# Startup and stage hand-over of a hybrid attention and SSD layer: x loaded whole, two sets of temporaries, one product order and one load order changed

## The reference, cut to what matters

```
h = rms_norm(x, norm_gain)                       # x: 1024 rows x 1024
proj = h @ w_in                                  # -> q, k, v, z, xBC, dt, gates
o_a = window_attention(q, k, v, ...)             # 16 heads, window of 128
y_s = ssd_mixer(conv(xBC), dt, ...)              # chunks of 64; B and C are part of xBC
branch_a = (o_a * silu(z_a)) @ w_attn_proj
branch_b = rms_norm(y_s * silu(z_s)) @ w_ssd_proj
out = x + (sigmoid(g_a) * branch_a + sigmoid(g_b) * branch_b) @ w_out
```

## Time and profile before

| what | value |
|---|---|
| time, median of 3 runs | 1417.9 us (1417.76 to 1418.82) |
| the profiled execution's own time | 1417.91 us |
| its span in the profile | 1416.1 us |
| PE busy, share of the span | 96% |
| DVE, ACT, POOL busy | 55%, 43%, 41% |
| mean granted clock of PE | 0.986 |

### The profile page before, as it was taken

One profiled execution on the slowest core, in us unless ns is written; L12 is line 12 of the kernel. 1 busy time (PEld: TensorE's weight loads), 2 busy tenths in 40 slices (PEclk: granted clock), 3 DMA queues, 4 the chain that ended last, 5 costly groups with the idle time before them and its releaser, 6 DMA issues.

```text
span 1416.1 us, 20612 instructions
## 1 busy us (share of the span) xinstructions
PE 1358.4 (96%) x7108; PEld 1088.0 (77%) x7108; DVE 782.6 (55%) x955; ACT 612.1 (43%) x1148; POOL 585.1 (41%) x344
## 2 busy tenths in 40 slices
PE   5698999999999979999999999999999999998999
PEld 4686777888888857888787878888768888776787
DVE  4775777676666455536554555555365554555311
ACT  5545444545444343435252535344356533323110
POOL 3443564445544423333333233333336666443321
PEclk9899999999999989999999999999999999999999
DMA  5331644422323276778666785869586265334431
GB/s 201 144 90 66 191 138 134 178 103 99 110 104 119 103 183 157 189 199 157 202 154 203 164 210 151 238 150 202 129 296 235 104 218 196 136 139 158 146 106 59
DMA packets 166500, 221.59 MB, mean 156 GB/s; under 512 B 7760, under 2 KB 127824, under 8 KB 166208
## 3 DMA queue, kind: packets, MB, share of 16 engines
q1 hardware_dynamic: 130640, 172.64, 43.0%
q10 hardware_dynamic: 35728, 48.37, 9.4%
q0 software_dynamic: 96, 0.13, 0.0%
HBM read 152.57 MB, written 63.31 MB: 152 GB/s over the span
## 4 chain that ended last, share of the span: by engine, by line
PE 84%; issue 5%; POOL 3%; DVE 3%; DMA 2%; ACT 2%; SPq 0%; ACTq 0%; POOLq 0%; DVEq 0%
PE F L180 37%; PE F L930 28%; PE F L1772 3%; PE M L1772 3%; PE M L1093 2%; PE M L1136 2%; DMA sb_early<-x_d 2%; POOL sb_res L1596 1%; PE F L1130 1%; PE F L1123 1%; PE F L1107 1%; PE M L1130 1%; PE M L1123 1%; PE F L1725 1%; PE F L899 1%
## 5 line engine op out<-in xcount | busy, mean ns | idle before, releaser
L180 PE MATMUL F<-sb_xb,sb_whl 128*128 128x512 f32 x1536 | 376.3, 402 | 0.0
L180 PEld LDWEIGHTS F<-sb_xb,sb_whl 128*128 128x128 f32 x1536 | 286.9, 188 | 75.2 <-issue 9.2
L192 POOL TENSOR_TENSOR sb_whl<-sb_wst,sb_whl 128x1024 fp32r<-128x1024 f32 x64 | 159.3, 2490 | 405.6 <-ACT sb_whl L189 405.3
L180 PE MATMUL F<-sb_X,sb_whl 128*128 128x512 f32 x1104 | 259.7, 396 | 5.9 <-issue 3.0
L180 PEld LDWEIGHTS F<-sb_X,sb_whl 128*128 128x128 f32 x1104 | 206.5, 187 | 58.5 <-issue 8.2
L930 PE MATMUL F<-sb_tv,sb_whl 128*128 128x512 f32 x1008 | 242.4, 396 | 2.3 <-DVE sb_acc L734 2.3
L930 PEld LDWEIGHTS F<-sb_tv,sb_whl 128*128 128x128 f32 x1008 | 189.2, 188 | 49.3 <-issue 3.1
L414 POOL TENSOR_TENSOR sb_whl<-sb_acc,sb_whl 128x512 fp32r<-128x512 f32 x103 | 145.7, 1421 | 135.8 <-ACT sb_whl L461 135.8
L930 PE MATMUL F<-sb_xb,sb_whl 128*128 128x512 f32 x756 | 187.6, 401 | 7.5 <-POOL sb_whl L414 5.7
L930 PEld LDWEIGHTS F<-sb_xb,sb_whl 128*128 128x128 f32 x756 | 142.7, 190 | 46.3 <-POOL sb_whl L414 7.6
L189 ACT ACTIVATE sb_whl<-sb_wst 128x1024 fp32r<-128x1024 f32 x64 | 67.6, 1058 | 198.4 <-DMA sb_wst<-w_units 97.1
(11 more groups left out here) (216 smaller groups left out, 1776.5 us busy)
## 6 DMA issues: line engine op xcount, KB each, us to landing
sb_wst<-w_units SPq DMA_DIRECT2D x64, 512.0 KB, 5.8
sb_acc<-cs_d SPq DMA_DIRECT2D x8, 2048.0 KB, 20.6
sb_wst<-w_units SPq DMA_DIRECT2D x12, 1024.0 KB, 4.9
x_d<-sb_res ACTq DMA_DIRECT2D x24, 512.0 KB, 2.7
sb_acc<-w_units SPq DMA_DIRECT2D x10, 1024.0 KB, 4.9
sb_acc<-x SPq DMA_DIRECT2D x16, 512.0 KB, 5.1
sb_early<-x_d SPq DMA_DIRECT2D x8, 1024.0 KB, 8.1
sb_acc<-ecs_d SPq DMA_DIRECT2D x16, 512.0 KB, 23.6
```

The lines of the kernel that those rows point to most:

```text
L180: last = nc.tensor.matmul(bank, weight(slot, wp, k), act(ap, k, half), start=(k == 0 and wp == 0 and ap == 0), stop=(k == NK - 1 and wp == 1))
L192: return nc.gpsimd.tensor_tensor(weights(slot, 1), raw_unit(slot), weights(slot, 0).bitcast(f32), ALU.subtract)
```

## The change

1. All eight tiles of x are loaded at once, into the part of `TV` that is written last. A row then lies in pieces of 128 numbers (512 bytes) with a stride, where it was one piece of 4 KB before. The order of the first loads changes too: tile 0, the v weights, dt, then tile 1.
2. `ttmp` becomes two sets, so `b12_copy(q)` waits for `t_lo` of q - 2.
3. Lists of the startup: PE starts the projections one tile later; ACT makes the v weights' high part of unit 0 ahead of the squares of tile 1; the low part of dt moves from POOL to DVE; POOL makes the first product's low part ahead of the last `t_lo`; `combine_x(3)` goes ahead of a `take_dt`, `v_copy(6)` ahead of a `split`.
4. In the last pair only, products 4 and 5 change places. PE's loop is one pair shorter and the last pair is written out.
5. SP's first tile of stage 2 is written out, and `bc` is loaded in it right behind `xb`, ahead of the weight unit and of `csb`. The other tiles keep their order.
6. `state` is cleared by POOL, behind its low parts of the weights, and PE waits for that only ahead of `off(0)`. PE's entry to stage 2 waits for `u2_done` in place of `c12_done`.

```diff
-        xrow, w = carve(acc_all, 2 * NK * VD, 3, DM)
+        ttmp2, w = carve(acc_all, 2 * NK * VD, 4, 4, P)
+        sums, w = carve(acc_all, w, 2, HALF)
...
-        ttmp, _ = carve(part_all, 0, 4, 4, P)
+        ttmp1, _ = carve(part_all, 0, 4, 4, P)
+        ttmp = (ttmp1, ttmp2)
...
+        def order(n):
+            return (0, 1, 2, 3, 5, 4, 6) if n == NPAIR - 1 else range(7)
...
+        def xrow(n):
+            rows = early.rearrange("p a (s k t) -> p (a s) k t", s=2, k=NK)
+            return rows[:, n % 4, :, (2 + n // 4) * P:(3 + n // 4) * P]
...
             load_x(0)
-            load_x(1)
             sp.dma_start(wst[:]..., a["w_units"][V0:V0 + 2]...).then_inc(v_in1, 16)
             sp.dma_start(dtraw[:], ...).then_inc(v_in1, 16)
-            load_x(2)
-            for n in range(3, NT):
-                sp.wait_ge(xt_done, n - 2)
+            load_x(1)
+            for n in range(2, NT):
                 load_x(n)
-                if n == 4:
-                    sp.wait_ge(v_lo, 3)
-                    load_raw(0)
+            sp.wait_ge(v_lo, 2)
+            load_raw(0)
...
             def b12_copy(q):
-                if q:
-                    act.wait_ge(t_lo, q)
+                if q >= 2:
+                    act.wait_ge(t_lo, q - 1)
...
             for q in range(4):
+                if q == 3:
+                    product_low(0, 0)
                 pool.wait_ge(t_hi, q + 1)
...
+                if n == 2:
+                    dve.wait_ge(v_hi, 3)
+                    nc.vector.tensor_tensor(vw[:, 1, :, 2 * P:VD], dtraw[:], vw[:, 0, :, 2 * P:VD].bitcast(f32),
+                                            ALU.subtract).then_inc(dt_lo, 1)
...
             for n in range(NT):
                 transpose_x(n)
-                if n == 1:
-                    pe.wait_ge(v_lo, 3)
-                if n >= 1:
-                    project_vdt(n - 1)
+                if n == 2:
+                    pe.wait_ge(v_lo, 2)
+                    pe.wait_ge(dt_lo, 1)
+                if n >= 2:
+                    project_vdt(n - 2)
+            project_vdt(NT - 2)
             project_vdt(NT - 1)
...
-            with nc.tensor.Fori(0, NPAIR - 8) as i:
+            with nc.tensor.Fori(0, NPAIR - 9) as i:
                 for idx in range(7):
                     product(idx, i, 1, 8)
+            for idx in range(7):
+                product(idx, 0, 0, NPAIR - 1)
...
                 sp.dma_start(xb[:], x_d[0:16, ...]...).then_inc(x2_in, 16)
+                if first:
+                    sp.wait_ge(prod, 7 * (NPAIR - 1) + 5)
+                    load_bc(j, at_j)
                 load_w(sp, B2 + 2, 4, j)
...
-            pe.wait_ge(c12_done, NPAIR)
+            pe.wait_ge(u2_done, NPAIR)
...
-            dve.wait_ge(c12_done, NPAIR)
-            nc.vector.memset(state[:], 0.0).then_inc(state_ready, 1)
+            dve.sem_inc(state_ready, 1)
...
+            pool.wait_ge(c12_done, NPAIR)
+            nc.gpsimd.memset(state[:], 0.0).then_inc(state_zero, 1)
```

More of the change, by code:

```diff
@@ L450, in split @@
             def split(n, idx):
-                if idx in (0, 4, 5):
+                if order(n)[idx] in (0, 4, 5):
                     act.wait_ge(raw_in[n % 2], 16 * (n // 2 + 1))
@@ L486, in _ @@
             t_high(3)
+            v_copy(NT - 2)
             split(0, 1)
-            v_copy(NT - 2)
             split(0, 2)
@@ L646, in _ @@
             post_a(NPAIR - 1)
+            act.wait_ge(prod, 7 * NPAIR - 1)
+            high(act, 0, 0, 0)
             act.wait_ge(prod, 7 * NPAIR)
-            high(act, 0, 0, 0)
             high(act, 1, 0, 0)
@@ L925, in product @@
                     pe.wait_ge(t_lo2, 1)
+                what = idx if c else order(n)[idx]
                 if idx >= 4:
-                    pe.wait_ge((u2_done, u3_done, c22_done)[idx - 4], at * c + (n + 1))
+                    pe.wait_ge((u2_done, u3_done, c22_done)[what - 4], at * c + (n + 1))
                 for k in range(4):
                     for wp, ap in ((0, 0), (0, 1), (1, 0)):
-                        last = nc.tensor.matmul(F[:, BANK[idx], :], ring(idx, wp)[:, k * P:(k + 1) * P], moving(idx, ap, k),
+                        last = nc.tensor.matmul(F[:, BANK[what], :], ring(idx, wp)[:, k * P:(k + 1) * P], moving(what, ap, k),
                                                 start=(idx < 4 and k == 0 and wp == 0 and ap == 0),
@@ L1041, in _, with load_bc, tile_loads @@
             sp.wait_ge(prod, 7 * (NPAIR - 1) + 2)
-            with nc.sync.Fori(0, NT) as j:
-                at_j = sp.snap(j * P)
+            def load_bc(j, at_j):
+                sp.wait_ge(yg_done, j * 4 + 1)
+                sp.dma_start(bc[:], x_d[16:24, :, ds(at_j, P)].rearrange("n p t -> p n t")).then_inc(bc_in, 16)
+            def tile_loads(j, at_j, first):
                 sp.wait_ge(sc_done, j * 4 + 1)
@@ L1067, in _ @@
                     load_w(sp, B2 + n, 4, j)
+            tile_loads(0, 0, True)
+            with nc.sync.Fori(1, NT) as j:
+                tile_loads(j, sp.snap(j * P), False)
         @block.tensor
@@ L1180, in _ @@
                 diag(1)
+                pe.wait_ge(state_zero, 1)
                 off(0)
```

77 lines of the change are left out of this document (44 added, 33 removed).

## The result

| kernel | time, median (range) | ratio to before, 95% interval |
|---|---|---|
| before | 1417.8 us (1414.1 to 1418.8) | 1 |
| changed | 1404.6 us (1403.7 to 1406.4), 4 runs | 0.991 (0.990 to 0.992) |
| forecast | 1402.6 us (1398.2 to 1409.5) | |

The kernel is faster by 13.2 us, and the interval of the ratio excludes 1. The profiled execution of the changed kernel has a span of 1403.3 against 1416.1, so 12.8 of it can be followed in the two traces. In what follows the lines have moved: L439 of before is L450, L699 is L722, L410 is L422, L930 is L960, L1093 is L1136, L1052 is L1087, L1057 is L1096, L1059 is L1076, L1249 is L1292, L1244 is L1287, L1258 is L1301 and L1433 is L1479.

A forecast was written before the change was run, and what follows sets the result against it. PE, busy 96% of the span, bounds the kernel, leaving its waits and low-clock stretches in the startup and stage 2's first tile. 11.2 + 4.1 = 15.3 us off 1417.9 gives 1402.6 us, range 1398.2 to 1409.5.

The forecast's parts named there:

- the loop: Startup, ACT, POOL and DVE per pair: `t_high` every 11.5 us, since DVE's row scaling waits for POOL's low part.
- Rival (C): Startup: x in 512-byte pieces loads at `csb`'s rate, tile 7 lands at 49, first product at 71.4; 1413.4 us, chance 0.06.
- Rival (D): Startup: PE's clock does not rise, first product about 9 later, pair 0 stays slow; 1423.1 us, chance 0.04.
- part 1: Startup: first product at 60.6 instead of 68.94 gains 8.3, faster products of pair 0 gain 2.9; 11.2 us together.
- What follows in pairs 0 to 3 hangs on products of PE and moves along: Products after the startup: later work shifts with PE, so the startup's 11.2 us is kept.
- part 2: Stage boundary: early `bc` removes PE's wait, normalisation is late next; gains 4.1 us, bounds 0 and 8.4.
- L1249 at 2.4: First tile of stage 2: sign of error if the two `causal` run undisturbed; over 5 us for two was expected.
- Its issue at 505.22 hangs on `w_lo` after the last product and stays: Stage boundary: `csb`'s issue time is unchanged by the early `bc`, so it lands at 525.5.
- The hold that I had put there: First tile of stage 2: POOL's L1433, ending at 527.7, holds DVE, so `causal(0)` ends at 528.8.
- rival (A): Stage boundary: no blocking of DVE by POOL, 4.3 us more gained; 1398.3 us, chance 0.12.
- Rival (B): Smaller gain: `norm_ready` 4 at 534 or later, or x and two projections 2 to 3 late; 1405.5 to 1409.5, chance 0.21.
- (E): Whole change: the loop's wait and `bc` give nothing; time within 3 of 1417.9 us, chance 0.03.

The follow-up runs named there:

- the second profile: The changed kernel run and profiled again without an edit; measured 1405.9 us, ratio 0.992 (0.989 to 0.994).
- the second profile of before: The kernel before, run and profiled again without an edit; measured 1417.9 us, ratio 1.000 (0.999 to 1.001).
- the boundary alone: Kernel before with only the product order, PE's entry, early `bc` and the clearing of `state` as changed; 1416.3 us, ratio 0.998 (0.997 to 1.000).

## Why the prediction was right, and where it was off

**Right: the loop and what it does to the second temporary.** The period was given as 11.5 and is 11.49; `t_high` was given at 24.7, 36.1, 47.6 and 55.6 and came 0.3 to 0.9 earlier. That DVE is held by POOL's instruction is shown from three sides. Taking the second temporary away changes nothing in the loop but the last pair. Cutting POOL's instruction frees DVE and shortens the period to 10.67, 9.49 and 8.15, although POOL works longer. With the cut, one temporary costs 10.7 us, some 1.5 of it by the clock. The trace agrees with what "SBUF — State Buffer" of the Trainium skill, section "SBUF: two separate sides", states of the two engines. That section also has the lock last for a whole instruction, and the cut shows it: DVE got in within POOL's 6.0 of four instructions, after waiting 0.3 (the scaling of tile 4 took 1.57 instead of 1.28; with one temporary 1.89, a wait of 0.6).

**Right, and a little early: the first product.** Given 60.6, measured 59.13. Row 7 was scaled at 48.2 where I had 49.1, the last three projections took 9.83 instead of 10.05, and the 0.5 for a slow one was not needed. The first projection (4.17 where I took 5.05) is not the reason: in the second profile it took 4.96, and the first product came at 58.84. Rival (C), slow pieces, fell (the eight loads landed 7.4 after their issue at the median). Its 71.4 did not follow from its own condition either: by my chain a row scaled at 49.1 gives a first product at 60.1, so one that lands at 49 gives it some 3 to 5 us later than that, an estimate from 1.5 for the squares and 1.3 to 3.4 for the scaling, and not 11. Pair 0 was not slow: 2.96 for its first product against 5.49. Rival (D), a clock that stays low in the startup, fell too.

**Off: the size of part 1, 11.2 forecast, 9.5 kept in the profiled execution.** The step that failed is "What follows in pairs 0 to 3 hangs on products of PE and moves along". After pair 0 PE was 12.4 ahead, 1.2 more than the sum had, since the first product was early. But DVE's work for pair 1 hung on ACT and was only 11.4 ahead. So PE's wait there grew from 1.34 to 2.29, and the clock fell after it: PE was 11.4 ahead at that product and 9.9 ahead after the slow matmuls. A second slow stretch cost 0.4 more. The second profile shows the same wait without the first fall, and there part 1 kept 11.3. That this is close to 11.2 is luck, for two misses cancel: PE was 12.6 ahead after pair 0, and pairs 1 and 2 took back 1.3. The forecast also took the length of a wait to decide over the clock, slow after 2.87 and not after 1.70. That does not hold: after the same 1.81 the matmuls were slow in both profiles of the changed kernel (4.58 and 4.52) and not in those of before (3.03).

**Off: part 2, 4.1 forecast, 0.7 kept.** The wait for `bc` went, and `norm_ready` 4 was late next, as given: PE idle 4.44 (given 4.2), and PE goes on 32.7 after the last product (given 531.7, which is 32.6 after 499.14). That agreement is luck, for two misses cancel in it, and the forecast's own sign of being wrong, "L1249 at 2.4", came. The step that failed is "Its issue at 505.22 hangs on `w_lo` after the last product and stays". `bc` was priced by itself, 1.6 us of transfer and 3.9 after the last product, and at nothing for its neighbours. It landed 7.6 after the last product (497.2), a store of z beside it took 5.9 instead of 4.5 at most, and SP, which waits for that store, issued `csb` 1.3 later. With `bc` late this is gone (3.8, no wait). So `csb` came at 28.7 after the last product instead of 26.4, 0.09 after POOL's L1479 had ended, and nothing held `causal`. In the second profile it was 27.4, also after POOL's end. The hold that I had put there appeared in the runs in which `csb` came before POOL's end, and there it cost 0.15 to 0.94; my sum had 2.1 for it.

Three more terms were too small. PE started 3.52 after the last product where I gave 2.4, since `xb` took 8.4 to land and not the least of the eight old times; in the other runs it started 2.6 to 3.9 after it. The 0.7 that I gave for an earlier entry had little ground: in the second profile of before PE was released by `xb` itself, 3.2 after the last product. The half unit behind the wait took 7.70 where the sum had 5.6 + 1.05 (6.84 in the second profile). And the waits of 1.26 for L1301 and 0.76 for `bc` in tile 1 were in no term. The first is the hold of DVE by POOL, which I had priced at `causal` and not looked for in the rest of the tile. The second profile kept 1.3 by the same count (from the last product to L1160 of tile 1 94.81, against 95.46 in the first and 96.16 before). In the boundary alone the first tile did give 3.8 of the 4.1, and later tiles took it back.

**The sum.** 10.2 in the first profile (9.5 + 0.7) and 12.6 in the second (11.3 + 1.3), in place of 15.3. The first profile's time was as near the forecast as it was because stage 3 took 2.6 less in it than in the first profile of before, which the executions do by themselves. Over the four executions the gain is 12.5 by the ratio, with an interval of 10.8 to 14.2, and 11.9 in the second measurement. So the forecast was 2 to 3 us too large, within its range. Of rival (A) the condition came true, no hold at `causal`, but not its time, since `csb` was late. Rival (B) had a smaller gain for other reasons: `norm_ready` 4 was not later against the last product, and x and the projections were not late; what it named rightly was DMA traffic at the boundary. (E) fell, since the gain is beyond what a measurement can't tell. One reading of the trace was too short, though nothing in the sum rests on it: "After 570 us it is PE without a break". The kernel before has waits of 3.5 us ahead of L1725 from 1037 us on and of 5.9 us between 1250 and 1330.

What stays open is why the granted clock falls after one wait of 2.3 us and not after another. "TensorE: Matmul & The Clock Gate" of the Trainium skill, section "Part 1: The HAM clock gate", states that the window in which the chip looks at activity runs freely and does not start with the kernel. The two profiles of one kernel fit that, and no run here tests it. Open are also the waits for `bc` in later tiles, and how much of `xb`'s lateness is due to `bc`: PE's entry came 2.6 to 3.5 after the last product with this startup whether `bc` was beside it or not.

## What to carry to other kernels

Before giving a buffer a second copy, ask what else stops in the same stretch: here DVE was held by the very POOL instruction whose end the buffer waited for, and the second copy paid only after that instruction was cut in four, 10.7 us with the cut and nothing that the times could tell without it. When a DMA is moved forward in a queue, price its neighbours again: here a store beside it landed at 5.9 instead of 3.8, and a load that waits for this store was issued 1.5 later. Count a gain again some tiles on: with the boundary alone, 3.8 us won in the first tile were gone by tile 7. And a queue that looks idle can be the worst place of all: behind a 1 MB store, with other loads under way, the same load landed after 34.9 instead of 5.1.

## What was not expected of the hardware

The clock after a short wait of PE is not the same in each execution. After 2.29 us of waiting, 12 matmuls took 4.58 in one and 3.03 in another profile of the same kernel. Over all runs with a wait of 2.2 to 2.3 in pair 1 they were slow (4.54 to 4.59) in six profiles and not (3.02 to 3.04) in five. After the wait of 1.81 in pair 2 they were slow (4.48 to 4.59) in eleven and not (3.03) in three, two of which are those of the kernel before. POOL's 2048 columns took 4.60 in one instruction and 6.0 in four beside a working DVE, 5.0 for the third pair. A 512 KB load in ACT's queue landed 5.1 after its issue in the first tile and 34.9 at the median over all, behind a 1 MB store, and the engine that issued it was held for 7.56 in tile 1.
